# Norms of the delta rule's last two heads by logarithm and exponential within the inverse, and two clears by GpSimd

## The reference, cut to what matters

```
def l2_norm(x):
    xf = x.astype(jnp.float32)
    return xf * lax.rsqrt(jnp.sum(xf * xf, axis=-1, keepdims=True) + EPS)

qkv = jax.nn.silu(causal_depthwise_conv(qkv, conv_w))
q = l2_norm(heads(q, GDN_DK))
k = l2_norm(heads(k, GDN_DK))
...
a_low = jnp.where(strict, jnp.einsum('bhncd,bhnsd->bhncs', k_beta, k) * decay, 0.0)
sol = lax.linalg.triangular_solve(eye + a_low, rhs, left_side=True, lower=True,
                                  unit_diagonal=True)
```

## Time and profile before

| | before |
|---|---|
| device time, runs of the kernel | 2230.69, 2233.72 and 10999.35 us, median 2233.72 |
| device time of the profiled execution | 2230.66 us |
| its span | 2228.8 us |
| PE busy | 1994.5 us (89%) |
| DVE busy | 996.6 us (45%) |
| ACT busy | 699.8 us (31%) |
| POOL busy | 335.5 us (15%) |
| mean granted TensorE clock | 0.951 of full |
| last matmul of the projection's sums ends | at 928.0 us |
| first instruction of the inverse stage | at 945.5 us |

### The profile page before, as it was taken

The page is one execution under the profiler, slowest core; times in us unless marked ns, Lnnn a source line. Parts: engine busy times, 40 slices in busy tenths (PEclk is TensorE's granted clock), DMA queues, the critical chain, the costliest instruction groups (busy, mean ns, idle before and its releaser), DMA issues. The chain is left out here.

```text
span 2228.8 us, 28821 instructions
## 1 busy us (share of the span) xinstructions
PE 1994.5 (89%) x11270; PEld 1490.2 (67%) x11270; DVE 996.6 (45%) x1385; ACT 699.8 (31%) x1091; POOL 335.5 (15%) x264
## 2 busy tenths in 40 slices
PE   5988994977886999668899999999999889999999
PEld 2756762322225777567788888888677777888887
DVE  3431434211115567866454433333587445333333
ACT  2432231201103444334433322222542544222232
POOL 1332210211113344034321000000200001000000
PEclk9999996999998999889999999999999899999999
DMA  8137027899982222111002222232222012222221
GB/s 345 48 132 272 14 67 284 328 423 425 422 348 77 67 87 93 59 43 35 2 29 95 86 95 94 96 100 95 85 76 76 1 48 88 101 94 93 96 95 47
DMA packets 64276, 287.53 MB, mean 129 GB/s; under 512 B 10248, under 2 KB 11560, under 8 KB 54840
## 3 DMA queue, kind: packets, MB, share of 16 engines
q1 hardware_dynamic: 55376, 271.15, 33.0%
q0 software_dynamic: 6256, 11.03, 1.3%
q10 hardware_dynamic: 2552, 4.05, 0.5%
HBM read 285.10 MB, written 14.71 MB: 135 GB/s over the span
## 5 line engine op out<-in xcount | busy, mean ns | idle before, releaser
L308 PE MATMUL ps<-t_hhi,t_whi 128*128 128x512 f32 x768 | 304.8, 397 | 2.8 <-POOL t_wlo L2665 1.6
L310 PE MATMUL ps<-t_hlo,t_whi 128*128 128x512 f32 x768 | 304.7, 397 | 0.0
L309 PE MATMUL ps<-t_hhi,t_wlo 128*128 128x512 f32 x768 | 302.5, 394 | 0.0
L2463 DVE TENSOR_TENSOR t_wlo<-ring,t_whi 128x1024 fp32r<-128x1024 f32 x132 | 163.9, 1242 | 244.4 <-ACT t_whi L2459 244.4
L2459 ACT ACTIVATE t_whi<-ring 128x1024 fp32r<-128x1024 f32 x132 | 139.3, 1055 | 322.8 <-PE ps L310 322.8
L1513 PE MATMUL ps<-w_up,hgT 128*64 128x512 f32 x576 | 145.6, 658 | 45.0 <-DMA w_up<-experts 45.0
L308 PEld LDWEIGHTS ps<-t_hhi,t_whi 128*128 128x128 f32 x768 | 144.3, 188 | 40.6 <-DVE t_hlo L2729 3.7
L309 PEld LDWEIGHTS ps<-t_hhi,t_wlo 128*128 128x128 f32 x768 | 144.4, 188 | 35.6 <-issue 1.0
L310 PEld LDWEIGHTS ps<-t_hlo,t_whi 128*128 128x128 f32 x768 | 144.1, 188 | 33.1
L308 PE MATMUL ps<-t_ahi,t_whi 128*128 128x512 f32 x352 | 137.0, 389 | 0.0
L309 PE MATMUL ps<-t_ahi,t_wlo 128*128 128x512 f32 x352 | 137.0, 389 | 0.0
(11 more groups left out here) (556 smaller groups left out, 3725.1 us busy)
## 6 DMA issues: line engine op xcount, KB each, us to landing
ring<-stream SPq DMA_DIRECT2D x276, 512.0 KB, 3.3
w_up<-experts SPq DMA_DIRECT2D x36, 2048.0 KB
mix<-experts SPq DMA_DIRECT2D x18, 1024.0 KB, 20.6
hn<-experts SPq DMA_DIRECT2D x18, 1024.0 KB, 21.6
yrow<-y_dram SPq DMA_DIRECT2D x4, 1024.0 KB, 8.0
tab<-table POOLq DMA_DIRECT2D x1, 2528.5 KB, 12.3
res<-xT ACTq DMA_DIRECT2D x1, 2048.0 KB, 18.9
h_dram<-mix SPq DMA_DIRECT2D x4, 512.0 KB, 10.3
```

Source lines behind the costliest of these rows:

```text
L308: pe.matmul(out, w_hi, a_hi, start=start, stop=False)
L309: pe.matmul(out, w_lo, a_hi, start=False, stop=False)
L310: return pe.matmul(out, w_hi, a_lo, start=False, stop=stop)
L2463: ve.tensor_tensor(w_lo[:, j % 2, :], ring[:, (B0 + j) % SLOTS, :], w_hi[:, j % 2, :].bitcast(F32), ALU.subtract).then_inc(blocks_done, 1)
```

## The change

The last two heads lose their square roots, reciprocals and multiplications in the projection stage. DVE only reads their four sums with EPS added, into `last_rs`, which is heads 4 to 7 of `hn`. ACT's last block of roots is gone. In the inverse stage ACT takes, behind the first pair's exponentials, one logarithm over all four (128x2048 elements) and one exponential with scale -0.5, which together give the inverse of the root. DVE multiplies Q and K of heads 6 and 7 by it, behind the first pair's `first_level` and ahead of its `keep_kd`. PE's `pair_products` of the last pair waits for these four multiplications. The two clears move from the head of DVE's list to the head of POOL's; ACT's first use of `mm_` and DVE's first `keep_kd` wait for them.

```diff
+        last_rs = hn[:, 4:8, :]
...
-                turns(act, one_turn, lambda before: [roots(u, before) for u in range(2)])
+                turns(act, one_turn, lambda before: None)
...
-                turns(ve, one_turn, lambda before: [normalise(u, before) for u in range(2)])
+                def last_means(before):
+                    for u in range(2):
+                        for j in range(2):
+                            ve.wait_ge(summed[u], before * 2 + j + 1)
+                            ve.tensor_scalar(last_rs[:, 2 * u + j, :], ps[:, 4 * u + 2 + j, :], EPS, None, ALU.add
+                                             ).then_inc(mean_read[u], 1)
+                turns(ve, one_turn, last_means)
...
                 def pair_products(p, u):
                     h = 2 * p + u
+                    if p == NPAIR - 1:
+                        pe.wait_ge(last_normed, 4)
...
-                        act.wait_ge(zeroed, 1)
+                        act.wait_ge(zeroed, 2)
...
-                for part in (exp_rows, exps, keep_t, keep_kv):
+                for part in (exp_rows, exps):
+                    for u in range(2):
+                        part(0, u)
+                act.activation(flat(last_rs), flat(last_rs), ACT.Ln).then_inc(last_logs, 1)
+                act.wait_ge(last_logs, 1)
+                act.activation(flat(last_rs), flat(last_rs), ACT.Exp, scale=-0.5).then_inc(last_inverse, 1)
+                for part in (keep_t, keep_kv):
...
+                pool.memset(mm_[:, :, :], 0.0).then_inc(zeroed, 1)
+                pool.memset(whole, 0.0).then_inc(zeroed, 1)
                 for u in range(2):
                     mask(0, 1, u)
...
-                ve.memset(mm_[:, :, :], 0.0).then_inc(zeroed, 1)
-                ve.memset(whole, 0.0).then_inc(zeroed, 1)
-                ve.wait_ge(zeroed, 2)
-                for part in (difference, decays, read_products, first_level, keep_kd):
+                for part in (difference, decays, read_products, first_level):
                     for u in range(2):
                         part(0, u)
+                ve.wait_ge(last_inverse, 1)
+                for u in range(2):
+                    for j, x in enumerate((Q, K)):
+                        h = HEADS - 2 + u
+                        ve.scalar_tensor_tensor(x[:, h, :], x[:, h, :], (P ** -0.5, 1.0)[j], last_rs[:, 2 * u + j, :],
+                                                ALU.mult, ALU.mult).then_inc(last_normed, 1)
+                ve.wait_ge(zeroed, 2)
+                for u in range(2):
+                    keep_kd(0, u)
```

More of the change, by code:

```diff
@@ L2043, in program @@
         S = {n: [sem(f"i_{n}{u}") for u in range(2)] for n in names}
-        zeroed = sem("i_zeroed")
+        zeroed, last_logs, last_inverse, last_normed = (
+            sem(f"i_{n}") for n in ("zeroed", "last_logs", "last_inverse", "last_normed"))
         NPAIR = HEADS // 2
```

## The result

The changed kernel took 2218.03 us (median of five runs, 2216.59 to 2219.91) against 2233.72 us before in the same session (median of five runs as well; one of them took 10999.35 us and is left out of the ratio, the other four took 2228.95 to 2235.25). The ratio is 0.9940 with a 95% interval of 0.9929 to 0.9952, so it is faster by 0.5 to 0.7%. Measured once more, with more runs on another occasion, the ratio was 0.9927 (0.9910 to 0.9944). The profiled execution took 2218.77 us with a span of 2216.9 us; before it was 2230.66 and 2228.8. That is 11.9 us less, and the forecast was 16.3.

The account below looks back on a forecast made before the run. PE was busy 89% of the span but stood idle behind DVE's tail between projection and inverse; -16.34 us plus four zero terms took the profiled 2230.66 us to 2214.3, given as 2215 us, range 2210 to 2220.

Parts of the forecast that it names:

- The tail: End of projection stage: DVE's reciprocals and multiplications after the four sums go, so the inverse stage starts 16.34 us earlier.
- ACT's logarithm and exponential: Behind the first pair's exponentials in the inverse: 6.40 us with two table loads, hidden before `keep_t`, cost 0.
- The multiplications: DVE, between `first_level` and `keep_kd`: four of 0.69 us, 2.77 us together, fit the 3.11 us gap, cost 0.
- Rival A: DVE's four multiplications take 1.18 us each and end late: 1.3 us lost, 2216 us; chance 0.08.
- the rule on two SBUF inputs: DVE multiplications ahead of `keep_kd`: instructions with two SBUF inputs contend with POOL instructions reading SBUF; POOL idle, so 0.69 us.
- The clears: Head of the inverse: moving two clears from DVE to POOL gains 0 and costs 0, about 0.9 us each.
- The last pair's wait: PE's `pair_products` of the last pair come dozens of microseconds behind the multiplications, so their wait costs 0.
- The row load: Start of the inverse: issued at about 929.2, it meets an empty queue and takes 3.4 us as before.
- Rival D: Start of the inverse held by a late ring load or row load: up to 3 us lost, 2217 us; chance 0.06.
- PE's clock: Inverse: products start at 2.4 GHz, turns again at 1.2 GHz; rival of staying up gains 1.3 us, 2213; chance 0.06.
- How far 16.3 us reach the end: Later stages: all 16.3 us reach the end, with 2.6 us either way for clock dips and about 3 between executions.
- The chances: Whole kernel, against a 2% threshold of 44.6 us: faster 0.01, within 2% 0.98, slower 0.01.

Follow-up runs that it names:

- twice: Changed kernel with a second multiplication, its result unread, behind each of the four on DVE; ratio 0.9933 to the kernel before the change.
- moved_root: Changed kernel with a square root on ACT and four reciprocals on DVE replacing logarithm and exponential, still in the inverse; ratio 0.9996 to the kernel before the change.
- clears_only: Kernel before the change with only the two clears moved from DVE to POOL; ratio 1.0008 to the unedited kernel.
- early_rows_table: Changed kernel plus the first pair's row loads and ACT's exponential table load issued in the projection stage; ratio 0.9918 to the kernel before the change.
- before: The kernel without the change, in its first trace; median 2233.72 us, profiled execution 2230.66 us.
- norms_only: Changed kernel with the two clears put back at the head of DVE's list; ratio 0.9939 to the kernel before the change.
- after: The changed kernel without further edits, in its first trace; median 2218.03 us, ratio 0.9940 to the kernel before the change.

## Why the prediction was right and wrong, by its steps

The mechanism came out as forecast, and every term of the sum at the seam with it. What failed is the last step, the chances; the way from the seam to the end was right within the range but had terms missing.

**The tail.** Right. 16.34 us were forecast, 16.47 measured (17.53 - 1.06), the same to a hundredth in both traces of the changed kernel. The fourth read starts 0.03 us behind PE's end instead of the 0.16 assumed. The seam itself is 0.28 us in both.

**ACT's logarithm and exponential.** Right: 1.91 us each for the 1.92 interpolated, table loads of 1.28 us, 3.61 us to spare for the 3.6 forecast.

**The multiplications.** Right: they take 0.69 us each and fit, with 0.65 us left where 0.34 was forecast, because they start 0.61 us apart. The forecast gave 0.67 us of lateness for free, 0.34 of it in the gap and 0.33 as ACT's own cover. `twice` tests the cover: the decayed K started 22.38 us behind PE's first product instead of 20.76, 1.6 us late, and ACT's copy 1.4 late, so the cover is 0.2 us. Rival A didn't occur: POOL was idle there, its next mask came at 954.47. Its mechanism is real all the same, as moved_root shows on this very instruction, 1.21 us against 0.69. The row that the prediction sets beside the rule on two SBUF inputs, 1.12 against 0.17 us, is of a copy with one such input: it shows that POOL matters, but it is no case of that rule. The multiplication in moved_root is one, and agrees.

**The clears.** Right: nothing gained (clears_only), nothing lost, 0.95 us each on POOL for 0.9 forecast.

**The last pair's wait.** Right: its products began at 1039.45, 88 us behind the last multiplication.

**The row load.** Right: 3.39 us from issue to ACT's start (930.91 to 934.30), as before. Rival D didn't occur, but by a small margin. In the changed kernel, too, the last ring load was issued just behind the start of the sums (926.64), and DMA was still busy until shortly before 930:

```profile
929.00:930.00 1.00, 0.90 (x3) 0.07 (x1) 0.75 (x2) 0.00 (x0) 0.00 (x0) 1.00 0.38 152
930.00:930.90 0.90, 0.00 (x0) 0.00 (x0) 0.63 (x1) 0.00 (x0) 0.00 (x0) 1.00 0.00 0
```

The row load was issued at 930.91, about one microsecond later. `early_rows_table` shows what lies on the other side of this margin: a load issued 0.6 us behind the ring load takes 4.9 us.

**PE's clock.** Right at this place: the products ran at a granted clock of 1.00 and their groups took 1.06 to 1.13 us, where the first of before took 2.04, and the turns ran at 0.50 again, 1.12 us for 16 matmuls.

**How far 16.3 us reach the end.** Here the sum of single traces was off: 11.9 us in the first pair of traces. The range had 2.6 us for the clock and 3 us for the execution, and the median, 2218.03, lies in it, 3 us above the forecast of 2215. Terms that were missing are the pace of the feed forward loops, 2.1 us each in one direction or the other, and the stretch ahead of the sums, which ended between 927.6 and 935.2 us in traces of kernels that are equal up to there. The 2.6 us given to the clock were small too: the stretch between the loops, at a mean clock of 0.96 in one trace and 0.98 in the other, differs by 4.8 us. Behind the seam, traces of kernels that differ by nothing but the clears are up to 9 us apart (1277.3 us from the first product to the end in norms_only, 1285.9 in after). The scan began at 1090.31 where 1088.7 was forecast; 1.9 us of that lie ahead of the sums, so the inverse itself came out as forecast. The prediction's last sign, stages behind 1100 longer by more than 3 us, came near (2.8 us), but it could not have told a wrong prediction from a right one: two traces of the changed kernel differ by 3.5 us there. The centre of the forecast was the profiled execution plus 0.7 us, and for a profiled execution of 2230.66 us that is too low: the runs of the kernel before lay at a median of 2232 to 2237 us in later sessions. Taken from the median of 2233.72, 2215 would be a gain of 18.7 us, more than the sum gave. The medians of the second measurement are 15.0 us apart (2232.63 and 2217.67). Its interval, 0.9910 to 0.9944, holds the seam's 16.5 us (a ratio of 0.9926), while that of the first, 0.9929 to 0.9952, just leaves them out, so whether a microsecond or two of the 16.5 is lost on the way to the end stays open.

**The chances.** This is the step that failed. The text took 2%, 44.6 us, for what a measurement can tell from no change, and on that ground put 0.98 on "within 2%" and only 0.01 on "faster", beside a sum that says 16.3 us faster. The measurement resolves 0.1 to 0.3%: the intervals here reach 0.11 to 0.26% to either side, and that of the change, 0.9929 to 0.9952, lies wholly below 1. What the prediction holds to be the mechanism didn't fail. A forecast of 0.7% faster, made from a stall of 17.5 us in which only one engine worked, should have been given as a gain that will be seen.

## What to carry to other kernels

A tail on one engine ahead of a barrier costs its whole length, however busy the kernel is on average; look for it as the longest idle time of the busiest engine that ends in a barrier, and then for a wait behind the barrier that is long enough for the work. Making the work shorter and moving it are worth more together than apart: here the method alone gave 7.4 us at the seam, the place alone 1.6 to 2.9 up to the scan, and both together 16.5 at the seam with nothing lost up to the scan. Judge such a change by the pieces of the trace around it, since single executions of a 2200 us kernel differed by 9 us in stages that nobody touched. And weigh a forecast gain against the spread of the measurement itself, not against a round 2%: here 0.7% was three to six times what the runs resolve.

## What was not expected of the hardware

- In the two feed forward loops TensorE streamed 128x512 matmuls at 231.1 or 233.3 ns from one to the next, both at a granted clock of 1.00, the same through a loop and changing between executions of one program (133.12 or 134.40 us for three turns). What sets it is open.
- The granted clock of the same stretch differed between executions of the same program. In the inverse the same 2384 matmuls took 134.7 us at a mean of 0.97, 136.0 at 0.96 and 137.6 at 0.95.
- A small load issued 0.6 us behind a load of 512 KB on the same queue took 4.9 us instead of 3.4.
- A DVE multiplication of two SBUF inputs took 1.21 us when POOL's mask was running as it started, and 0.69 us with POOL idle (moved_root).
